# Overflow blocks of a mixture of experts: 32 tokens on four column tiles in place of 64 on two

## The chip, the cores and the metric

The kernel runs on one core of a Trainium2 chip. The metric is the device time of one execution in microseconds (us). Before the change three runs took 2112.33, 2118.11 and 2120.79 us, median 2118.11.

## What is computed

The program is one transformer block (gated token mixer, then a mixture of 32 experts) followed by a second block of two layers (pooling and gated delta rule, each with a feed-forward part). There are 256 tokens of width 1024, all in fp32. The part that the change touches is the mixture of experts:

```python
logits = (xt @ w_router + b_router)            # 256 tokens, 32 experts
top_logits, top_idx = lax.top_k(logits, 4)     # each token goes to 4 experts
top_w = jax.nn.softmax(top_logits, axis=-1)
# for each expert e and the tokens that chose it:
gate, up = jnp.split(xb @ w_gu[e] + b_gu[e], 2, axis=-1)   # 1024 -> 2 x 1024
gate = jnp.minimum(gate, 7.0); up = jnp.clip(up, -7.0, 7.0)
act = (up + 1) * (gate * jax.nn.sigmoid(1.702 * gate))
y[token] += top_w * (act @ w_dn[e] + b_dn[e])              # 1024 -> 1024
```

The number of tokens of an expert depends on the data. With the inputs of this case the router gives experts 2, 16, 27 and 29 more than 64 tokens: 90, 99, 89 and 78. Expert 21 has exactly 64, all others fewer.

## The kernel before

Every engine has its own program, and they meet through semaphores. TensorE (PE) multiplies, VectorE (DVE) makes selection matrices and the clipped activations, ScalarE (ACT) makes the sigmoid and copies, and SyncE (SP) issues the loads of the experts' weights: 12 units of 1 MiB for each expert (8 of gate and up, 4 of down), 384 in all, in a fixed order. The 8 slots of the gate-and-up weights hold one expert's; the down weights have two sets of 4 slots. A slot is loaded again when PE has used it in the expert's last block (`w_used`).

The loop `experts` (L614 to L628) runs on PE, DVE and ACT alike: 16 turns of two experts (j = 0, 1). For each expert the engine reads its number of tokens (L620) and runs an inner loop over b = 1, 2, 3 (L621). A turn with more than 64·b tokens runs `overflow`, a block of 64 tokens. Any other turn only waits until the engine's own earlier steps are done, adds the steps it skips to the semaphore, and goes on (L627). Then `last_block` handles tokens 0 to 63, for every expert. An overflow block comes ahead of it and uses the same resident weights.

A block on PE: the bias (L1171), then gate and up (L1182): for each of 8 slices of 128 inputs four matmuls of 512 columns, 64 tokens stationary, so that the array works as two column tiles of 64. Then the scatter of the previous block's result (L1231), a transposition of the selection matrix (L1207) and of the activations (L1199), and down (L1220), 16 matmuls of 512 columns, two tiles again. An overflow block gathers its tokens first (L1163), while `last_block` gathers those of the next pair (L1155). On DVE a block is limit (L2420, L2421), product with the sigmoid (L2425), the activations (L2429) and the copy of their transposition (L2434); an overflow block begins with the slots (L2401, L2408) and the copy of the gathered tokens (L2413). On ACT it is the sigmoid (L1790), the copy of the transposed selection (L1794) and that of the result (L1799).

An fp32 matmul of the program is two weight loads and two matmuls in the trace.

Of the kernel before, what the change touches and what calls it, by code (L numbers as in the profile page):

```python
# [8 lines left out]
I32 = mybir.dt.int32  # L9
# [4 lines left out]
P = 128  # L14
# [6 lines left out]
KCH = 64  # L21
BLK = 64
EG = 2

PE_MAIN = ("gate_up", "scattered", "next_gathered", "act_T0", "act_T1", "spread_T")
PE_OVER = ("gathered", "gate_up", "scattered", "spread_T", "act_T0", "act_T1", "down")
# [3 lines left out]
DVE_OVER = ("slots0", "slots1", "spread0", "spread1", "tokens", "gate_min", "up_clip", "gated", "act0", "act1",  # L32
            "act_T0", "act_T1")
ACT_FIRST = ACT_OVER = ("sigmoid", "spread_T", "down")
ACT_SECOND = ("sigmoid", "staged_in", "spread_T", "down")

def build(nc, A, out):
# [17 lines left out]
    GTAPS = A["gdn_conv_2"].shape[1]  # L55
    NBLK = S // BLK
    assert NT == 2 and D == 1024 and HEADS == ND and NG == ND and NE == 32

    ctx = ExitStack()
    with ctx:  # L60
# [28 lines left out]
        level = sb("level", [P, 6, P])  # L89
        slot_row = sb("slot_row", [P, NBLK, 2, BLK])  # L90
        slot_int = g2_bc[:, 0:NBLK * 2 * BLK].bitcast(I32)
        inv_pos = sb("inv_pos", [P, 16])
# [471 lines left out]
        pad_end = apad[:, :, :].rearrange("p m t -> p (m t)")[:, len(WINDOWS) * 3 * P:]  # L564
        xg_o = pad_end[:, 0:512].rearrange("p (d s) -> p d s", s=BLK)
        slots_o = pad_end[:, 512:640].rearrange("p (t s) -> p t s", s=BLK)
        bgu_parts = w7[0:96, 1024:2048].bitcast(BF16)
# [12 lines left out]
        class Steps:  # L580
# [3 lines left out]
            def __init__(self, sem_, mains, over, base):  # L584
                self.sem, self.base, self.over_len = sem_, base, len(over)
                overs = (NBLK - 1) * len(over)
                self.first = [j * overs + sum(len(m) for m in mains[:j]) for j in range(EG)]
                self.per = EG * overs + sum(len(m) for m in mains)
                self.main = [{n: overs + i + 1 for i, n in enumerate(m)} for m in mains]
                self.over = {n: i + 1 for i, n in enumerate(over)}  # L590

            def did(self, eng, where, step, pairs_ago=0):

                g, j, b = where
                base = self.base + self.first[j] - pairs_ago * self.per
                if isinstance(b, int):
                    eng.wait_ge(self.sem, g * self.per + (base + self.main[j][step]))
                else:
                    eng.wait_ge(self.sem, g * self.per + b * self.over_len + (base - self.over_len + self.over[step]))

            def started(self, eng, where, less=0):

                g, j, b = where
                base = self.base + self.first[j] - less
                if isinstance(b, int):
                    eng.wait_ge(self.sem, g * self.per + (base + (NBLK - 1) * self.over_len))
                else:
                    eng.wait_ge(self.sem, g * self.per + b * self.over_len + (base - self.over_len))

# [79 lines left out]
        def _(pool):  # L689
# [38 lines left out]
            for i in range(6):  # L728
# [5 lines left out]
                masked(v, [[2 * s, k], [0, s]], s - 1, -1, ALU.is_ge, 0.0)  # L734
            link(nc.gpsimd.iota(slot_int, pattern=[[BLK, NBLK], [0, 2], [1, BLK]], base=0,
                                channel_multiplier=0))
            link(nc.gpsimd.tensor_copy(slot_row[:, :, :, :].rearrange("p b r s -> p (b r s)"), slot_int))
            link(nc.gpsimd.iota(slot_int[:, 0:16], pattern=[[1, 16]], base=1, channel_multiplier=0))
# [112 lines left out]
        def _(pe):  # L851
# [307 lines left out]
            def gather(s_):  # L1159

                for d in range(ND):
                    for t in range(NT):
                        ins = mm(bX[:, d * BLK:(d + 1) * BLK], h2_tok[:, t, d * P:(d + 1) * P], s_[:, t, :],  # L1163
                                 start=t == 0, stop=t == NT - 1)
                step(ins)
# [8 lines left out]

            def gate_and_up(w, x, last):

                for kt in range(ND):
# [6 lines left out]
                    if kt == ND - 1:  # L1184
                        step(ins)
                    elif last:
                        ins.then_inc(w_used, 1)

            def weights(w, u):
# [20 lines left out]

            def down(w, last):
                for n, v in enumerate(DN_ORDER):
# [9 lines left out]
                    if last:  # L1222
                        ins.then_inc(w_used, 1)
                    elif n == 3:
                        step(ins)

# [26 lines left out]
            def overflow(w):  # L1253
                DV.did(pe, w, "slots1")
                AC.started(pe, w, less=1)
                gather(slots_o)
                gate_up_bias()
                DV.did(pe, w, "tokens")
                gate_and_up(w, lambda kt: xg_o[:, kt, :], False)
                AC.started(pe, w)  # L1260
                scatter(spread_T, y_blk)
                spread_transposed(w, spread)
                activation_T(w, 0, bG)
                activation_T(w, 1, bU)
                down(w, False)

            def last_block(w):
# [3 lines left out]
                if j == 0:  # L1271
                    AC.did(pe, (w[0], EG - 1, 0), "staged_in", pairs_ago=1)
                gate_and_up(w, lambda kt: xg[kt // UK][:, kt % UK, j * BLK:(j + 1) * BLK], True)
                AC.started(pe, w)
# [7 lines left out]
                spread_transposed(w, spread)  # L1282
                down(w, True)

# [368 lines left out]
        def _(act):  # L1653
# [134 lines left out]
            def act_block(w, st, y):  # L1788
                DV.did(act, w, "gate_min")
                f(g_sig, g_min, ACT.Sigmoid, scale=SWIGLU).then_inc(moe_act, 1)  # L1790
                if isinstance(w[2], int) and w[1] == EG - 1:
# [232 lines left out]
        def _(dve):  # L2024
# [371 lines left out]
            def find_slots(dst, e, b):  # L2396

                row = slot_row[:, 0, 0, :] if isinstance(b, int) else \
                    slot_row[:, bass.ds(b, 1), 0, :].rearrange("p o s -> p (o s)")
                for t in range(NT):  # L2400
                    step(v.tensor_scalar(dst[:, t, :], row, place[:, t, bass.ds(e, 1)], None, ALU.is_equal))  # L2401

            def find_spread(dst, e, b):

                row = slot_row[:, 0, :, :] if isinstance(b, int) else \
                    slot_row[:, bass.ds(b, 1), :, :].rearrange("p o r s -> p (o r) s")
                for t in range(NT):
                    step(v.tensor_scalar(dst[:, t, :].rearrange("p (r s) -> p r s", r=2), row,  # L2408
                                         place[:, t, bass.ds(e, 1)], gate_of[:, t, bass.ds(e, 1)],
# [7 lines left out]

            def limited(w):
                PE.did(dve, w, "gate_up")
                step(v.tensor_scalar(g_min, banks[5][:, :], LIMIT, None, ALU.min))  # L2420
                step(v.tensor_scalar(u_clip, banks[6][:, :], LIMIT, -LIMIT, ALU.min, ALU.max))  # L2421

            def gated(w):
                AC.did(dve, w, "sigmoid")
                step(v.tensor_tensor(g_act, g_min, g_sig, ALU.mult))  # L2425
                DV.did(dve, w, "gated")
                for i in range(2):
                    cs = slice(i * 256, (i + 1) * 256)
# [9 lines left out]
            for e in range(EG):  # L2438
                for t in range(NT):
                    n[0] += 1  # L2440
                    v.tensor_scalar(slots[:, t, e * BLK:(e + 1) * BLK], slot_row[:, 0, 0, :],
                                    place[:, t, e:e + 1], None, ALU.is_equal).then_inc(dve_step, 1)
# [12 lines left out]
            def overflow(w):  # L2455
# [4 lines left out]
                PE.did(dve, w, "gathered")  # L2460
                copy_tokens(xg_o)
                limited(w)
                gated(w)
                copy_act_T(w)

            def last_block(w):
# [5 lines left out]
                find_spread(spread, e + j, 0)  # L2472
                limited(w)
                gated(w)
                PE.did(dve, w, "next_gathered")
# [471 lines left out]
```

## Time and profile before

| | us |
|---|---|
| median of three runs (lowest, highest) | 2118.11 (2112.33, 2120.79) |
| the profiled execution's own time | 2111.71 |
| its span, first to last instruction | 2110.0 |
| PE busy | 1948.9 (92%) |
| DVE, ACT, POOL busy | 908.0, 469.5, 70.5 |
| first bias matmul of the experts to the end of the last down matmul | 362.6 to 1383.0 |

The experts take about 1020 of the 2110 us. The last line is read from the list of PE's instructions in order of time. A busy PE is not PE at its peak, since a matmul's record is longer than the distance to the next one. Register, branch and semaphore instructions aren't counted as busy; rows named PEldq or PEq are those of PE's sequencer.

### The profile page before, as it was taken

Reading aid. Unit: us, or ns where it says so; the run is one execution under the profiler, and the core shown is the slowest. Engines: PE = TensorE matmul, PEld = TensorE weight load, DVE = VectorE, ACT = ScalarE, POOL = GpSimd, SP = SyncE. Lnnn points to the kernel's source line nnn. Section 1 sums busy time; section 2 is a strip of 40 time slices with the busy share of each in tenths; the row PEclk is TensorE's granted clock in tenths of the full one; section 3 lists DMA queues with packets and bytes.
Section 4 is the critical chain, followed back from the end, with each engine's and each line's share of the span. In section 5 each row is a group of like instructions: output and inputs, shape, how many; then the busy total and the mean of one; then the engine's idle time right before and its main releaser. Section 6 shows DMA issues by size and latency. Waiting matters only on the chain. (4 is left out here: it accounts for less than half of the span.)

```text
span 2110.0 us, 28553 instructions
## 1 busy us (share of the span) xinstructions
PE 1948.9 (92%) x10917; PEld 1222.1 (58%) x10918; DVE 908.0 (43%) x1444; ACT 469.5 (22%) x557; POOL 70.5 (3%) x128
## 2 busy tenths in 40 slices
PE   4999896999999999999999999989999998999998
PEld 2859774433333333333333333358987997878986
DVE  3799644111111111111111121176556787876554
ACT  2223101000000000100000000024543643334542
POOL 2000002000000000000000000010000000020000
PEclk9999997999999999999999999999999989999999
DMA  9794834959999999899999985936555620054552
GB/s 360 246 324 156 300 126 146 417 216 422 421 422 422 422 422 422 332 423 422 422 422 422 408 344 226 401 107 213 180 198 164 202 96 1 1 173 162 189 190 80
DMA packets 143604, 581.37 MB, mean 276 GB/s; under 512 B 10520, under 2 KB 12552, under 8 KB 94281
## 3 DMA queue, kind: packets, MB, share of 16 engines
q1 hardware_dynamic: 136384, 564.43, 68.6%
q0 software_dynamic: 3040, 11.02, 1.7%
q10 hardware_dynamic: 4105, 4.86, 0.7%
q8 instruction: 54, 0.88, 0.2%
q14 instruction: 21, 0.17, 0.0%
HBM read 579.23 MB, written 1.05 MB: 275 GB/s over the span
## 5 line engine op out<-in xcount | busy, mean ns | idle before, releaser
L1182 PE MATMUL bank<-ring,area 128*64 128x512 f32 x2048 | 459.2, 597 | 28.0 <-DMA ring<-in_w_gu 27.6
L1182 PEld LDWEIGHTS bank<-ring,area 128*64 128x64 f32 x2048 | 144.0, 137 | 325.3 <-issue 235.5
L924 PE MATMUL bank<-area_r,ring_r 128*128 128x256 f32 x992 | 282.6, 285 | 9.3 <-DVE area_r L2155 7.1
L926 PE MATMUL bank<-area_r,ring_r 128*128 128x256 f32 x992 | 281.5, 284 | 0.0
L927 PE MATMUL bank<-area_r,ring_r 128*128 128x256 f32 x992 | 281.5, 284 | 0.0
L289 DVE TENSOR_TENSOR ring_r<-ring,ring_r 128x2048 fp32r<-128x2048 f32 x90 | 205.8, 2291 | 149.8 <-ACT ring_r L286 148.1
L2420 DVE TENSOR_SCALAR area<-bank 128x512 f32<-128x512 f32 x36 | 24.9, 692 | 539.6 <-PE bank L1182 539.6
L286 ACT ACTIVATE ring_r<-ring 128x2048 fp32r<-128x2048 f32 x92 | 175.7, 1913 | 179.4 <-PE bank L927 152.2
L924 PEld LDWEIGHTS bank<-area_r,ring_r 128*128 128x128 f32 x992 | 191.3, 193 | 12.1 <-DVE area_r L2155 7.3
L1220 PE MATMUL bank<-area 128*64 128x512 f32 x864 | 192.5, 594 | 0.6 <-DVE area L2434 0.5
L926 PEld LDWEIGHTS bank<-area_r,ring_r 128*128 128x128 f32 x992 | 191.3, 193 | 0.0
L927 PEld LDWEIGHTS bank<-area_r,ring_r 128*128 128x128 f32 x992 | 191.2, 193 | 0.0
L1790 ACT ACTIVATE area<-area 128x512 f32<-128x512 f32 x36 | 22.7, 631 | 532.6 <-DVE area L2420 532.6
L1220 PEld LDWEIGHTS bank<-area 128*64 128x64 f32 x864 | 62.5, 137 | 115.7 <-issue 112.1
L924 PE MATMUL bank<-ring_r,area_r 128*128 128x512 f32 x304 | 118.8, 391 | 1.0 <-DVE area_r L2302 1.0
L926 PE MATMUL bank<-ring_r,area_r 128*128 128x512 f32 x304 | 118.3, 389 | 0.0
L927 PE MATMUL bank<-ring_r,area_r 128*128 128x512 f32 x304 | 118.3, 389 | 0.0
L2185 DVE SCALAR_TENSOR_TENSOR area<-apad,cols,area 128x256 f32<-128x256 f32 x240 | 96.1, 479 | 0.3 <-DVE area L2085 0.2
L1155 PEld LDWEIGHTS bank<-area 128*128 128x128 f32 x544 | 64.6, 195 | 26.0 <-issue 13.9
L1494 PE MATMUL bank<-area 128*128 128x128 f32 x560 | 69.9, 285 | 10.0 <-issue 5.4
L1799 ACT ACTIVATE area<-bank 128x512 f32<-128x512 f32 x36 | 21.5, 597 | 247.3 <-PE bank L1220 247.3
L1494 PEld LDWEIGHTS bank<-area 128*128 128x128 f32 x560 | 66.9, 198 | 13.1 <-issue 7.3
(341 smaller groups left out, 2177.8 us busy)
## 6 DMA issues: line engine op xcount, KB each, us to landing
ring<-in_w_gu SPq DMA_DIRECT2D x256, 1024.0 KB, 21.1
area<-in_w_dn SPq DMA_DIRECT2D x96, 1024.0 KB, 21.0
ring<-in_mlp_w SPq DMA_DIRECT2D x64, 1024.0 KB, 5.4
ring<-in_w_dn SPq DMA_DIRECT2D x32, 1024.0 KB, 19.5
ring<-in_w_in SPq DMA_DIRECT2D x24, 1024.0 KB, 6.3
ring<-in_gdn_w_in SPq DMA_DIRECT2D x16, 1024.0 KB, 5.5
area<-in_w_mod SPq DMA_DIRECT2D x12, 1024.0 KB, 8.6
ring<-in_w_mod SPq DMA_DIRECT2D x8, 1024.0 KB, 17.1
```

The lines of the kernel that those rows point to most:

```text
L286: nc.scalar.activation(unit_high(i), raw, ACT.Copy).then_inc(w_high, 1)
L289: nc.vector.tensor_tensor(unit_low(i), raw, unit_high(i), ALU.subtract).then_inc(w_split, 1)
L924: ins = mm(out_, a_[0], b_[0], start=start, stop=False)
L926: mm(out_, a_[0], b_[1], start=False, stop=False)
L927: return mm(out_, a_[1], b_[0], start=False, stop=stop)
L1155: ins = mm(bk[:, d * P:(d + 1) * P], h2_tok[:, t, (UK * dh + d) * P:(UK * dh + d + 1) * P], slots[:, t, :], start=t == 0, stop=t == NT - 1)
L1182: ins = mm(bk[hf * BLK:(hf + 1) * BLK, :], x(kt), block_u[:, c:c + BANK], start=False, stop=kt == ND - 1)
L1220: ins = mm(bT[hf * BLK:(hf + 1) * BLK, :], actT[:, 2 * i + k, fh * BLK:(fh + 1) * BLK], block_u[:, c:c + BANK], start=n == 0 and k == 0, s ...
L1494: return lambda bk, i, h: mm(bk[:, i * P:(i + 1) * P], l[:, h, :], r[:, h, :], start=True, stop=True)
L1790: f(g_sig, g_min, ACT.Sigmoid, scale=SWIGLU).then_inc(moe_act, 1)
L2185: v.scalar_tensor_tensor(acc[:, m, :], apad[:, m, j:j + S], col("conv_w", j * ND + m), acc[:, m, :], ALU.mult, ALU.add).then_inc(conv_step, 1)
L2420: step(v.tensor_scalar(g_min, banks[5][:, :], LIMIT, None, ALU.min))
```

## The change

`BLK` stays 64 for `last_block`. Overflow blocks have the new width `OBLK` = 32, and the inner loop runs over b = 2 to 7 (six turns in place of three), with `n_tok - b * OBLK > 0` as its condition. In an overflow block PE works as four column tiles of 32: gate and up is 64 matmuls of 256 columns in place of 32 of 512, and in down the two halves of the contraction go to tiles of their own, whose sums the scatter adds. The activations of a block are then 128 partitions by 256, so that DVE and ACT handle 256 elements in each operation in place of 512, and two transpositions do in place of four. `last_block` is unchanged.

```diff
-                    with eng.Fori(1, NBLK) as b:
-                        with eng.If(n_tok - b * BLK > 0):
+                    with eng.Fori(OVER0, OVER1) as b:
+                        with eng.If(n_tok - b * OBLK > 0):
                             overflow((g, j, b))
                         with eng.Else():
 
                             steps.started(eng, (g, j, b))
                             eng.sem_inc(steps.sem, steps.over_len)
                     last_block((g, j, 0))
...
+    OVER0, OVER1 = BLK // OBLK, S // OBLK
...
+            def over_bias():
+
+                for part, bk in ((0, bG), (1, bU)):
+                    for q in range(4):
+                        c = part * D + q * (D // 4)
+                        mm(bk[q * OBLK:(q + 1) * OBLK, 0:D // 4], expert_sel[:, 0:OBLK], bgu_parts[:, c:c + D // 4],
+                           start=True, stop=False)
+
+            def over_gate_and_up(w):
+
+                for kt in range(ND):
+                    block_u = weights(w, kt)
+                    for part, bk in ((0, bG), (1, bU)):
+                        for q in range(4):
+                            c = part * D + q * (D // 4)
+                            ins = mm(bk[q * OBLK:(q + 1) * OBLK, 0:D // 4], xg_o[:, kt, :], block_u[:, c:c + D // 4],
+                                     start=False, stop=kt == ND - 1)
+                step(ins)
+
+            def over_activation_T(w):
+
+                DV.did(pe, w, "act")
+                pairs = e_act[:, 0:D // 4].rearrange("p (f k) -> p k f", k=2)
+                for k in range(2):
+                    ins = mm(bG[:, k * P:(k + 1) * P], pairs[:, k, :], ident[:, :], is_transpose=True,
+                             start=True, stop=True)
+                step(ins)
+
+            def over_down(w):
+
+                DV.did(pe, w, "act_T")
+                for n, v in enumerate(DN_ORDER):
+                    block_u = weights(w, NGU + n)
+                    for k in range(2):
+                        for hf in range(2):
+                            r, c = (2 * hf + k) * OBLK, k * D + hf * BANK
+                            ins = mm(bT[r:r + OBLK, :], actT[:, k, v * OBLK:(v + 1) * OBLK],
+                                     block_u[:, c:c + BANK], start=n == 0, stop=n == 3)
+                step(ins)
...
             def overflow(w):
                 DV.did(pe, w, "slots1")
                 AC.started(pe, w, less=1)
                 gather(slots_o)
-                gate_up_bias()
+                over_bias()
                 DV.did(pe, w, "tokens")
-                gate_and_up(w, lambda kt: xg_o[:, kt, :], False)
+                over_gate_and_up(w)
                 AC.started(pe, w)
                 scatter(spread_T, y_blk)
                 spread_transposed(w, spread)
-                activation_T(w, 0, bG)
-                activation_T(w, 1, bU)
-                down(w, False)
+                over_activation_T(w)
+                over_down(w)
...
                 PE.did(dve, w, "gathered")
-                copy_tokens(xg_o)
-                limited(w)
-                gated(w)
-                copy_act_T(w)
+                step(v.tensor_copy(xg_o, banks[4][:, 0:ND * OBLK].rearrange("p (d s) -> p d s", s=OBLK)))
+                limited(w, D // 4)
+                gated(w, D // 4)
+                PE.did(dve, w, "act_T")
+                step(v.tensor_copy(actT[:, 0:2, :], banks[5][:, 0:2 * P].rearrange("p (j s) -> p j s", s=P)))
```

The rows of `place` numbers that the slots are compared with, the step counts of the semaphores and the sigmoid's width follow from this.

PE's program at the start of the overflow block of the first expert of a pair, before: the count is read, the loop entered, the condition tested, and then come gather (L1163), bias (L1171) and the first slices of gate and up.

```order
988 L620 TENSOR_LOAD counts
989 L620 ISA x2
990 L621 UNCONDITIONAL_BRANCH
991 L621 ISA
992 L622 COMPARE_AND_BRANCH
994 L608 ISA
995 L1163 MATMUL bank4<-apad,area 128x64 x16
996 L1171 MATMUL bank5<-area,expert_sel 64x512 x2
997 L1171 MATMUL bank6<-area,expert_sel 64x512 x2
1000 L1182 MATMUL bank5<-ring,apad 64x512 x2
1001 L1182 MATMUL bank6<-ring,apad 64x512 x2
```

The same place now, where gate and up is L1207 and the bias L1197:

```order
992 L625 COMPARE_AND_BRANCH
994 L611 ISA
995 L1166 MATMUL bank4<-apad,area 128x32 x16
996 L1197 MATMUL bank5<-area,expert_sel 32x256 x4
997 L1197 MATMUL bank6<-area,expert_sel 32x256 x4
1000 L1207 MATMUL bank5<-ring,apad 32x256 x4
1001 L1207 MATMUL bank6<-ring,apad 32x256 x4
```

The order is the same; each pair of matmuls of 512 columns has become four of 256. A pair's loop has 296 matmuls in PE's program before and 372 after. What a turn without a block executes stands at the end of PE's overflow block, before:

```order
1032 L1220 MATMUL bank7<-area 64x512 x8
1033 L622 UNCONDITIONAL_BRANCH
1034 L608 ISA
1035 L624 UNCONDITIONAL_BRANCH
1036 L621 REGISTER_ALU
1037 L621 COMPARE_AND_BRANCH
1038 L606 ISA
```

And now:

```order
1031 L1228 MATMUL bank7<-area 32x512 x8
1032 L625 UNCONDITIONAL_BRANCH
1033 L611 ISA
1034 L627 UNCONDITIONAL_BRANCH
1035 L624 REGISTER_ALU
1036 L624 COMPARE_AND_BRANCH
1037 L609 ISA
```

The instructions of a turn are the same ones; they are executed six times for an expert in place of three.

## Rows read from the trace of the kernel before

**Rows 1.** The page, clock and memory traffic in 40 slices of 52.75 us.
```profile
PEclk9999997999999999999999999999999989999999
...
GB/s 360 246 324 156 300 126 146 417 216 422 421 422 422 422 422 422 332 423 422 422 422 422 408 344 226 401 107 213 180 198 164 202 96 1 1 173 162 189 190 80
```

**Rows 2.** PE in order of time, 476 to 534 us: start, length, line, [idle before].
```profile
477.15 0.61 PE L1171 MATMUL bank<-area,expert_sel 96*64 96x512 bf16 x4
477.58 13.91 PE L1182 MATMUL bank<-ring,area 128*64 128x512 f32 x64
...
503.91 0.62 PE L1171 MATMUL bank<-area,expert_sel 96*64 96x512 bf16 x4
...
530.37 0.61 PE L1171 MATMUL bank<-area,expert_sel 96*64 96x512 bf16 x4
```

**Rows 3.** The bias line L1171, 605 to 818.15 us: ns min/median/max, first and last start.
```profile
L1171 PEld LDWEIGHTS bank<-area,expert_sel x31: 106/107/112, 610.4 to 818.1; 96*64 96x64 bf16 x31
```

**Rows 4.** PE in order of time around expert 2's overflow block, 414 to 452 us.
```profile
419.58 3.79 PE L1163 MATMUL bank<-apad,area 128*128 128x64 f32 x32
423.29 0.62 PE L1171 MATMUL bank<-area,expert_sel 96*64 96x512 bf16 x4
424.24 13.95 PE L1182 MATMUL bank<-ring,apad 128*64 128x512 f32 x64 [0.32 <-DVE apad L2413]
438.12 1.99 PE L1231 MATMUL bank<-area 64*128 64x512 f32 x8
...
445.41 3.61 PE L1220 MATMUL bank<-area 128*64 128x512 f32 x16
450.69 0.62 PE L1171 MATMUL bank<-area,expert_sel 96*64 96x512 bf16 x4 [1.67 <-DVE area L2401]
```

**Rows 5.** Turns without a block, L627, 720 to 730 us, then 445 to 452 us.
```profile
L627 PEldq EVENT_SEMAPHORE  x3: 51/51/51, 726.3 to 728.5; - x3
...
L627 PEldq EVENT_SEMAPHORE  x2: 51/51/51, 449.1 to 450.2; - x2
```

**Rows 6.** PE in order of time, 700 to 762 us.
```profile
728.99 0.62 PE L1171 MATMUL bank<-area,expert_sel 96*64 96x512 bf16 x4 [0.18 <-DVE area L2401]
```

**Rows 7.** Instructions by line, DVE and PE.
```profile
L2420 DVE TENSOR_SCALAR area<-bank 128x512 f32<-128x512 f32 x36 | 24.9, 692 | 539.6 <-PE bank L1182 539.6
...
L2434 DVE COPY area<-bank 128x256 f32<-128x256 f32 x72 | 26.9, 414 | 1.0 <-PE bank L1199 1.0
```

**Rows 8.** Line L1038, 121 to 126 us, then L1163, 418 to 425 us.
```profile
L1038 PE MATMUL bank<-area,cond x24: 592/592/617, 121.4 to 124.5; 128*32 128x512 f32 x24
L1038 PE MATMUL bank<-norm_bc,cond x8: 592/592/617, 121.5 to 124.5; 128*32 128x512 f32 x8
...
L1163 PE MATMUL bank<-apad,area x32: 275/275/323, 419.6 to 423.1; 128*128 128x64 f32 x32
```

**Rows 9.** Stretches: length, busy us of PE, PEld, DVE, ACT, POOL; clock; DMA share, GB/s.
```profile
97.00:100.00 3.00, 0.05 (x4) 0.08 (x8) 2.86 (x7) 0.00 (x0) 0.00 (x0) 1.00 0.27 101
...
100.50:103.90 3.40, 3.40 (x24) 1.07 (x19) 3.40 (x10) 0.00 (x0) 0.00 (x0) 0.50 0.00 0
...
1892.50:1894.70 2.20, 0.04 (x1) 0.07 (x1) 1.43 (x2) 2.20 (x3) 0.33 (x1) 1.00 0.71 199
...
1895.90:1899.30 3.40, 3.40 (x10) 2.66 (x9) 0.00 (x0) 0.00 (x0) 0.00 (x0) 0.50 0.96 353
...
450.70:453.70 3.00, 3.00 (x16) 1.14 (x18) 0.98 (x5) 1.28 (x1) 0.00 (x0) 1.00 0.00 0
```

**Rows 10.** Branches of PE's sequencer, whole run (L622: condition; L618: back to next pair).
```profile
L622 PEldq COMPARE_BRANCH  x100: 77/208/2143, 357.9 to 1355.3; - x100
...
L618 PEldq COMPARE_BRANCH  x17: 76/208/412, 356.1 to 1378.6; - x17
```

**Rows 11.** DMA queues, 340 to 405 us, then 470 to 1380 us: packets, MB, share.
```profile
q8 instruction: 6, 0.10, 0.6%
...
q14 instruction: 2, 0.02, 0.0%
```

More of the change, by code:

```diff
@@ L22 @@
 BLK = 64
+OBLK = 32
 EG = 2
 PE_MAIN = ("gate_up", "scattered", "next_gathered", "act_T0", "act_T1", "spread_T")
-PE_OVER = ("gathered", "gate_up", "scattered", "spread_T", "act_T0", "act_T1", "down")
+PE_OVER = ("gathered", "gate_up", "scattered", "spread_T", "act_T", "down")
 DVE_MAIN = ("spread0", "spread1", "gate_min", "up_clip", "gated", "act0", "act1", "next_tokens", "next_row",
@@ L585, in __init__ @@
                 self.sem, self.base, self.over_len = sem_, base, len(over)
-                overs = (NBLK - 1) * len(over)
+                overs = (OVER1 - OVER0) * len(over)
                 self.first = [j * overs + sum(len(m) for m in mains[:j]) for j in range(EG)]
@@ L598, in did @@
                 else:
-                    eng.wait_ge(self.sem, g * self.per + b * self.over_len + (base - self.over_len + self.over[step]))
+                    eng.wait_ge(self.sem, g * self.per + b * self.over_len + (base - OVER0 * self.over_len + self.over[step]))
             def started(self, eng, where, less=0):
@@ L1173, in gate_up_bias, with gate_and_up @@
                            start=True, stop=False)
-            def gate_and_up(w, x, last):
+            def gate_and_up(w, x):
                 for kt in range(ND):
@@ L1185, in gate_and_up @@
                         step(ins)
-                    elif last:
+                    else:
                         ins.then_inc(w_used, 1)
+            def over_bias():
[30 more added lines that the diff above has]
+                step(ins)
             def weights(w, u):
@@ L1209, in spread_transposed, with down @@
                 step(ins)
-            def down(w, last):
+            def down(w):
                 for n, v in enumerate(DN_ORDER):
@@ L1221, in down @@
                                      block_u[:, c:c + BANK], start=n == 0 and k == 0, stop=n == 3 and k == 1)
[L1222 to L1225, printed above, removed]
+                    ins.then_inc(w_used, 1)
             def scatter(st, y, last=False):
@@ L1282, in last_block @@
                 spread_transposed(w, spread)
-                down(w, True)
+                down(w)
             pe.wait_ge(moe_act, 3)
@@ L1789, in act_block @@
                 DV.did(act, w, "gate_min")
-                f(g_sig, g_min, ACT.Sigmoid, scale=SWIGLU).then_inc(moe_act, 1)
+                wide = BANK if isinstance(w[2], int) else D // 4
+                f(g_sig[:, 0:wide], g_min[:, 0:wide], ACT.Sigmoid, scale=SWIGLU).then_inc(moe_act, 1)
                 if isinstance(w[2], int) and w[1] == EG - 1:
@@ L2396, in find_slots @@
             def find_slots(dst, e, b):
-                row = slot_row[:, 0, 0, :] if isinstance(b, int) else \
-                    slot_row[:, bass.ds(b, 1), 0, :].rearrange("p o s -> p (o s)")
+                row = main_row[:, 0, :] if isinstance(b, int) else \
+                    over_row[:, bass.ds(b, 1), :].rearrange("p o s -> p (o s)")
                 for t in range(NT):
@@ L2403, in find_spread @@
             def find_spread(dst, e, b):
-                row = slot_row[:, 0, :, :] if isinstance(b, int) else \
-                    slot_row[:, bass.ds(b, 1), :, :].rearrange("p o r s -> p (o r) s")
+                row = main_row if isinstance(b, int) else \
+                    over_row[:, bass.ds(b, 1), :].to_broadcast([P, 4, OBLK])
                 for t in range(NT):
-                    step(v.tensor_scalar(dst[:, t, :].rearrange("p (r s) -> p r s", r=2), row,
+                    step(v.tensor_scalar(dst[:, t, :].rearrange("p (r s) -> p r s", s=row.shape[2]), row,
                                          place[:, t, bass.ds(e, 1)], gate_of[:, t, bass.ds(e, 1)],
@@ L2440, in _ @@
                     n[0] += 1
-                    v.tensor_scalar(slots[:, t, e * BLK:(e + 1) * BLK], slot_row[:, 0, 0, :],
+                    v.tensor_scalar(slots[:, t, e * BLK:(e + 1) * BLK], main_row[:, 0, :],
                                     place[:, t, e:e + 1], None, ALU.is_equal).then_inc(dve_step, 1)
@@ L2472, in last_block @@
                 find_spread(spread, e + j, 0)
-                limited(w)
-                gated(w)
+                limited(w, BANK)
+                gated(w, BANK)
                 PE.did(dve, w, "next_gathered")
```

40 lines of the change are left out of this document (21 added, 19 removed).

## The prediction, made before the changed kernel ran

> **What bounds the kernel now.** I read the page's slices first, to see in which stage the change lies. The experts fill slices 7 to 26; memory moves 422 GB/s in most of them and the granted clock is full [rows 1]. Whether PE or memory sets the pace there shows in PE's list in order of time, at the start of each block's bias. Where nothing is waited for, blocks follow each other by 26.76 and 26.46 us, mean 26.6, and gate and up takes 13.91 us [rows 2]. From 610.4 to 818.1 us there are seven such distances, 29.7 us each [rows 3]. That is memory's pace: 12 units of 1.049 MB are 12.58 MB, at 422 GB/s 29.8 us. So PE has 3.1 us of slack per expert, but only while it isn't late. Memory-bound blocks are eight before expert 16's overflow and five before expert 27's, 13 in all; in the others PE catches up after an overflow block, during which the weights' slots couldn't be freed. The waits for memory sum to 13 × 3.1 = 40 us. Every microsecond that PE gains or loses outside those blocks counts in full.
>
> **Turns of the loop.** The change adds three turns without a block for nearly every expert. The last turn's semaphore instruction starts 2.2 us after the first's of three, so that a turn takes PE's sequencer 1.12 us [rows 5]. Now three of them fit: the third's is at 728.5, the next bias starts at 728.99, with PE idle for 0.18 us [rows 5, 6]. The sequencer runs ahead of the queued down matmuls by just what three turns need, and nothing is left to hide three more. Each of the 27 steps between experts without an overflow grows by 3 × 1.12 = 3.4 us: 91 us. The first expert has the same in front: 3.4. DVE and ACT take six turns too, but PE's end last, since DVE's slots wait for PE's turns as it is. PE's distance becomes 26.6 + 3.4 = 30.0 us, just over memory's 29.8: the 40 us of waits go. I take the remainder of them as nothing; it may be 3.
>
> **The blocks.** Run through the reference's router, the inputs give 90, 99, 89 and 78 tokens for experts 2, 16, 27 and 29. At 32 tokens from 64 on, these are 1 + 2 + 1 + 1 = 5 blocks in place of 4. No count lies so near 64 or 96 that rounding would move it, except expert 21's 64, which needs no block in either form unless a token moves.
>
> An overflow block now spans 419.6 to 450.69, 31.1 us [rows 4]. Its parts:
> - Gather, bias, copy of tokens: 419.58 to 424.24, 4.7 us. The gather's 32 records stand 0.11 us apart for 64 columns each [rows 8], so narrower columns don't shorten it; the spacing is the loading of 128 stationary columns. The token copy falls from 512 to 256 elements, from about 692 to 414 ns [rows 7]: −0.3.
> - Gate and up: four column tiles run at once in this trace, 32 records of 512 columns from 121.4 to 124.5, eight groups 0.43 us apart [rows 8], 0.107 us for each. With 256 columns I take half, 0.053; 128 records are 6.9, with the tail 7.1 against 13.95 [rows 4]: −6.9. The bounds are this and 0.11 a record as in the gather, 14.2, no gain. I take the four-tile row, since the shape of the tiles is the same and only the columns are fewer.
> - From its end to down: now 3.7 us (438.19 to 441.93), a chain of DVE, ACT and DVE over 512 elements. By halves it would be 3.0, but PE has 2.4 us of scatter and transposed selection [rows 4], then two transpositions and a copy of 0.4, 3.4 in all: −0.3.
> - Down: 32 records of 512 columns, 0.107 each by [rows 8], 3.4 plus tail 0.2, against 7.1 (from 441.93 to 449.02, its last half in [rows 4]): −3.4.
>
> A block so loses 10.9 us, and is 18.5 long. Behind it stand the turns that are left. They start only when down is done (449.1), 1.1 us apart [rows 5], and the bias waits for them; the gap after down is 1.67 us now with two turns [rows 4] and becomes 5.1 with five. For experts 2, 27 and 29: −10.9 + 3.4 = −7.5, three times −22.5. Expert 16 has a second block: DVE's slots wait for the first one's down, 0.7, and 18.5, 19.2 together; its four turns cost 2.3 more than two. −10.9 + 19.2 + 2.3 = +10.6.
>
> **The clock.** The gaps at the end of every expert are now 0.2 us at most. They become 3.1 to 3.6, and 3.9 to 5.1 after the overflow blocks. After a gap of 3.0 us (97.0 to 100.0) the granted clock is 0.50 for 3.4 us, from 100.5; after one of 2.2 us it is too, from 1895.9 [rows 9]. These levels are 1.2 and 2.4 GHz. I find ten idle gaps of 2.2 us or more in the run, and a stretch at the low level begins in or right after each. After the 1.67 us behind the overflow block the clock stays at 1.00 [rows 4, 9]. So most of the new gaps will be followed by 3.4 us in which half the work is done, 1.7 us lost, less where the gap itself reaches into the stretch. Bounds: none of 31, 0; all at 1.7, 53. I take 25 of 31 at 1.5: +38. Memory has nothing to hide it with, since PE is the bound by then.
>
> **Sum.** 91 + 3.4 − 22.5 + 10.6 − 40 + 38 = +80.5 us. Against the profiled execution's own time of 2111.7 that is 2192; that execution is 6.4 us under the median of 2118.1, which would give 2199. I predict 2195. Outside the experts nothing changes that any stage waits for.
>
> **A rule against the loop.** The condition's branch on PE takes 208 ns in the median and 2143 at most; the branch back over the whole pair, 76 to 412 [rows 10]. The queue that brings PE's program moves six packets around the first pair and none during the later ones [rows 11], so the loop's code stays at hand after its first pass. The Trainium skill, "Runtime: NRT & Kernel Launch", Instruction fetch mechanics, gives PE an instruction memory of 128 KiB, but also says that a taken branch whose target isn't in the current two-page window forces a fetch. By that, a loop of six packets would miss at each jump, and the trace disagrees: the long branch back costs no more than the short ones. The changed pair has 372 matmuls in place of 296, a quarter more code. If six packets were all that is kept, jumps would miss again.
>
> **Rivals.**
> - *The clock holds.* The gaps repeat, but between them PE is busy for 26 us. Same sum without its last term: +42.5, 2154 to 2161. Against it stand all ten long gaps. Chance 0.17.
> - *The turns hide, and the kernel is faster.* Place: the sequencer under the down matmuls. If it entered the turns earlier, since the queue takes more, they would cost nothing, no gap would open, and the blocks' −10.9 × 4 + 19.2 = −24 would be left, of which memory-bound stretches take a few back: −20, 2092. With t the cost of a turn that shows, the loss is about 56·t (3t for 14 late experts, for the first, for three after blocks, 2t for expert 16, none for the 13 with slack), so it decides below 0.4 us a turn. The trace has 1.12 and an idle of 0.18, which says that the cover is used up. Chance 0.05.
> - *Four tiles don't run abreast at 256 columns.* Each of five blocks is 7 longer in gate and up and up to 3.4 in down: +52 on the forecast, 2245. Against it: L1038. Chance 0.06.
> - *The loop's code no longer stays.* One jump per expert at 2143 in place of 208 ns: 32 × 1.9 = 61 us more, 2255, twice that with two jumps. This is the rule's case, priced from [rows 10]. Chance 0.07.
> - The forecast itself: 0.62. Something else of either sign: 0.03.
>
> The range is 2152 to 2215: its lower end is the rival of the steady clock, its upper one all gaps at 1.7 us, taken from the median. About 0.5% (11 us) can be told from no change. Faster 0.06, same 0.03, slower 0.91.
>
> **What would show it.** PE's list of the changed kernel: biases 30 us apart plus what the clock takes, 31 to 32 where a low stretch follows; PE idle of 3.1 to 3.6 us before nearly every bias, with a turn as the releaser; six semaphore instructions of a turn 1.12 us apart; almost no waits of gate and up for the weights; memory's traffic under 422 GB/s in all of the stage; the page's clock below 9 tenths in the experts' slices; in five overflow blocks gate and up of 7.1 us and down of 3.6. The prediction is wrong if biases stand under 29.9 us apart (turns hidden), if the clock is 1.00 throughout the experts (its term gone), or if overflow gate and up takes 14.

## The result: 5.5% slower, and the profile after

The changed kernel takes 2234.47 us in the median of four runs (2228.16 to 2238.63), the one before 2117.73 (2112.33 to 2120.79); ratio 1.0552, 95% interval 1.0519 to 1.0585. The forecast was 2195 with 2152 to 2215: the direction and the mechanism hold, the time lies 20 us above the range. The profiled execution has a span of 2236.9 us and took 2238.63, the slowest of its four, while the profiled one of before (2111.71) was faster than all four timed ones of its kernel, so that the two profiles differ by 126.9 us and the medians by 116.7. Of all executions below, one (of the kernel with three turns, 2260.92 us at a mean granted clock of 0.83 in place of 0.97) was a slow one, and the ratios leave it out.

The page of the changed kernel, first PE's busy share and the granted clock in 40 slices of 55.9 us, then traffic, then gate and up of the last blocks:

```profile
PE   4999878888988898988898889898999998999998
...
PEclk9999896899999999999999999999999998999999
...
GB/s 361 246 303 133 281 120 212 352 236 398 391 388 389 412 386 380 170 326 379 396 399 390 393 248 394 238 273 115 200 188 193 188 164 1 1 114 168 186 195 87
...
L1185 PE MATMUL bank<-ring,area 128*64 128x512 f32 x2048 | 502.4, 653 | 0.0
L1185 PEld LDWEIGHTS bank<-ring,area 128*64 128x64 f32 x2048 | 163.0, 153 | 330.0 <-issue 328.7
```

None of the experts' slices has 422 GB/s any more; [rows 1] have it nearly throughout, and gate and up never waits for it: before, that line was idle 27.6 us for the weights, now nothing. Its mean matmul is 653 ns against 597. The clock's row in tenths hides what happens, since it rounds down and the same 9 stands for 1.00 and 0.92; a window query is needed. PE in order of time, 474 to 560 us:

```profile
489.51 3.61 PE L1263 MATMUL bank<-area 128*64 128x512 f32 x16
496.23 1.06 PE L1174 MATMUL bank<-area,expert_sel 96*64 96x512 bf16 x4 [3.11 <-PEq L630]
497.08 15.00 PE L1185 MATMUL bank<-ring,area 128*64 128x512 f32 x64
...
517.27 7.09 PE L1263 MATMUL bank<-area 128*64 128x512 f32 x32
527.88 1.07 PE L1174 MATMUL bank<-area,expert_sel 96*64 96x512 bf16 x4 [3.52 <-DVE area L2441]
528.72 16.24 PE L1185 MATMUL bank<-ring,area 128*64 128x512 f32 x64
```

The gaps ahead of the bias are the forecast 3.1 and 3.5 us; before there was none at 503.91 and 530.37 [rows 2]. But gate and up takes 15.00 and 16.24 in place of 13.91. The sequencer's turns (L630, 521 to 528 us), six, 1.12 us apart:

```profile
L630 PEldq EVENT_SEMAPHORE  x6: 51/51/51, 521.8 to 527.4; - x6
```

The clock around two gaps, columns as in [rows 9]; the last row is nearly the whole range of the experts:

```profile
524.40:527.90 3.50, 0.02 (x2) 0.03 (x3) 0.28 (x2) 0.60 (x1) 0.00 (x0) 0.81 1.02 424
527.90:533.40 5.50, 5.50 (x16) 1.86 (x18) 0.97 (x5) 1.28 (x1) 0.00 (x0) 0.50 0.95 380
533.50:537.00 3.50, 3.50 (x18) 1.14 (x16) 0.00 (x0) 0.00 (x0) 0.00 (x0) 1.00 0.82 276
557.30:560.40 3.10, 0.05 (x2) 0.06 (x4) 0.32 (x2) 0.58 (x1) 0.00 (x0) 1.00 1.01 420
560.70:564.10 3.40, 3.40 (x12) 1.02 (x10) 0.00 (x0) 0.00 (x0) 0.00 (x0) 0.50 1.02 424
...
380.00:1480.00 1100.00, 970.20 (x5070) 385.79 (x5068) 175.11 (x451) 87.83 (x141) 0.65 (x1) 0.92 0.87 351
```

After the gap of 3.1 us the clock is at 1.2 GHz for 3.4 us. With the gap of 3.5 it is low from inside the gap (the mean of 0.81 puts the fall at 526.6) to 533.4, 6.8 us. Each of the 31 gaps ahead of a last block, from the second expert on, has a low stretch in or behind it: 17 of 3.4 us, 13 of 6.8, and one of 10.2 at a gap of 8.7 us. Of the 26 gaps of 3.1 to 3.5 us, 11 have the long one.

**Where the 126.9 us of the profiles are.** I take from PE's list each expert's last block, from bias to the end of down (26.62 us where nothing disturbs it), and what lies between two of them.

| part | before | after | difference |
|---|---|---|---|
| start of the experts | 362.6 | 371.9 | +9.4 (3.4 are turns) |
| 27 steps between experts without an overflow | 1.6 | 94.7 | +93.1 |
| 4 steps with overflow blocks | 124.0 | 120.8 | −3.3 |
| excess of the 32 last blocks over 26.62, waits for memory | 40.9 | 0 | −40.9 |
| the same, low clock | 2.0 | 67.7 | +65.7 |
| after the experts | 727.0 | 729.9 | +2.9 |

The profile shows 27.6 of the 40.9 us as idle, since a matmul's record is longer than the distance to the next one.

### The profile page after: what moved, and what is told of

It is laid out like the page before. It is cut to its first block and busy times, and to the rows that moved or that the text cites. A ratio compares the mean times of both kernels' runs of the same rounds, so it can differ in the third digit from the quotient of the medians.

```text
span 2236.9 us, 31252 instructions
## 1 busy us (share of the span) xinstructions
PE 1996.7 (89%) x11393; PEld 1254.6 (56%) x11394; DVE 903.7 (40%) x1446; ACT 471.2 (21%) x561; POOL 70.8 (3%) x129
## 5 line engine op out<-in xcount | busy, mean ns | idle before, releaser
L1185 PE MATMUL bank<-ring,area 128*64 128x512 f32 x2048 | 502.4, 653 | 0.0
L1185 PEld LDWEIGHTS bank<-ring,area 128*64 128x64 f32 x2048 | 163.0, 153 | 330.0 <-issue 328.7
L2461 DVE TENSOR_SCALAR area<-bank 128x512 f32<-128x512 f32 (+1 forms) x37 | 24.3, 656 | 552.7 <-PE bank L1185 507.2
L1263 PE MATMUL bank<-area 128*64 128x512 f32 x768 | 171.1, 594 | 0.1
L1830 ACT ACTIVATE area<-area 128x512 f32<-128x512 f32 (+1 forms) x37 | 22.2, 601 | 623.8 <-DVE area L2461 623.8
L1174 PE MATMUL bank<-area,expert_sel 96*64 96x512 bf16 x128 | 31.0, 579 | 121.1 <-DVE area L2441 61.9
L1263 PEld LDWEIGHTS bank<-area 128*64 128x64 f32 x768 | 55.5, 137 | 102.5 <-issue 98.9
L1174 PEld LDWEIGHTS bank<-area,expert_sel 96*64 96x64 bf16 x128 | 5.6, 130 | 149.2 <-DVE area L2441 75.9
L2448 DVE TENSOR_SCALAR area<-slot_row,place,gate_of 128x128 f32<-128x128 f32 (+1 forms) x74 | 22.2, 342 | 158.8 <-PEq L630 158.8
L1158 PEld LDWEIGHTS bank<-area 128*128 128x128 f32 x544 | 65.3, 197 | 25.9 <-issue 13.7
```

The lines of the kernel that those rows point to most:

```text
L1158: ins = mm(bk[:, d * P:(d + 1) * P], h2_tok[:, t, (UK * dh + d) * P:(UK * dh + d + 1) * P], slots[:, t, :], start=t == 0, stop=t == NT - 1)
L1174: mm(bk[hf * BLK:(hf + 1) * BLK, :], expert_sel[:, :], bgu_parts[:, (2 * part + hf) * BANK:(2 * part + hf + 1) * BANK], start=True, stop=F ...
L1185: ins = mm(bk[hf * BLK:(hf + 1) * BLK, :], x(kt), block_u[:, c:c + BANK], start=False, stop=kt == ND - 1)
L2461: step(v.tensor_scalar(g_min[:, cs], banks[5][:, cs], LIMIT, None, ALU.min))
```

## The experiments

Each was timed together with the kernel before, whose medians were 2115.5 to 2116.8 us in these rounds, and ratios are to that. Lines moved by an edit are named by what they do.

**Three turns, narrow blocks.** `OVER1` is 5, so that the loop runs over b = 2 to 4.

```diff
-    OVER0, OVER1 = BLK // OBLK, S // OBLK
+    OVER0, OVER1 = BLK // OBLK, 5
```

> The changed kernel with its loop cut to three turns (b = 2 to 4, enough for the 99 tokens of the largest expert, not for inputs with over 160). Theory A (the turns make the loss: 3.4 us of sequencer time per expert, and a lower clock after each gap): the gaps between experts are 0.2 us again, the clock is 1.00 in the experts, waits for memory come back (about 13 blocks of 3 us), five narrow blocks of some 19.4 us stand in place of four of 29.4, and the time is 2098 to 2105. Rival B (the narrow blocks themselves cost more than they give, by four tiles at once or by their larger code): the time stays over 2118 although the gaps are gone.

2118.08 us, ratio 1.0008 (0.9993 to 1.0023). The gaps and the 116 us are gone, so the loss is the three added turns'. But the gain of 11 to 18 us that theory A wanted didn't come either: the time is the one that rival B named, so the narrow blocks take back what they give. The trace says how, in two ways (expert 2's block, then expert 27's):

```profile
425.97 4.49 PE L1166 MATMUL bank<-apad,area 128*128 128x32 f32 x32
430.39 0.62 PE L1197 MATMUL bank<-area,expert_sel 96*32 96x256 bf16 x8
431.07 9.34 PE L1207 MATMUL bank<-ring,apad 128*32 128x256 f32 x128
...
1205.41 7.85 PE L1207 MATMUL bank<-ring,apad 128*32 128x256 f32 x96
1213.74 1.07 PE L1207 MATMUL bank<-ring,apad 128*32 128x256 f32 x16 [0.47 <-DMA ring<-in_w_gu]
1216.23 1.07 PE L1207 MATMUL bank<-ring,apad 128*32 128x256 f32 x16 [1.42 <-DMA ring<-in_w_gu]
```

Narrow gate and up takes 9.3 us here (8.4 and 9.6 in the two others that don't wait for weights), not 7.1. And experts 16 and 27 come at the end of stretches that memory sets: their narrow block uses up the weights faster than they arrive and waits for them itself. The clock of this kernel in the first of the two blocks:

```profile
425.97:428.80 2.83, 2.83 (x28) 2.83 (x26) 0.00 (x0) 1.88 (x2) 0.00 (x0) 1.00 1.01 423
428.80:435.60 6.80, 6.74 (x61) 3.90 (x64) 0.42 (x1) 0.00 (x0) 0.00 (x0) 0.50 0.67 282
435.70:440.00 4.30, 4.30 (x84) 2.47 (x80) 0.00 (x0) 0.00 (x0) 0.00 (x0) 1.00 0.00 0
```

It falls in the middle of a gather in which PE's records have no gap.

**Six turns, wide blocks.** The kernel before with its loop over six turns; the last three are never taken.

```diff
+    TURNS = 6
...
-                    with eng.Fori(1, NBLK) as b:
+                    with eng.Fori(1, 1 + TURNS) as b:
```

The step counts and the row of slot numbers follow from it.

> The kernel before with 64-token blocks, its loop run over six turns, of which the last three never have a block (the row of slot numbers is stored once and broadcast). Theory A: the whole loss and more is in the turns. 27 steps between experts grow by 3.4 us (92), the four after blocks by 3.4 (14), the first by 3.4, the waits for memory go (-40), and the low clock after 31 gaps costs 2.1 each (65 to 70): +135, 2250. Rival B (a part of the loss is the narrow blocks' or their code's): +90 or less, 2210.

2246.64 us, ratio 1.0632 (1.0613 to 1.0651). Turns alone cost 131 us; theory A's 135 is met, rival B's 90 isn't. The narrow blocks give back some 12 by the medians, 14 if each kernel is set against the one before of its own round. The gap and the slow gate and up are those of the changed kernel, without a narrow block anywhere:

```profile
494.92 1.06 PE L1172 MATMUL bank<-area,expert_sel 96*64 96x512 bf16 x4 [3.14 <-PEq L628]
495.77 16.52 PE L1183 MATMUL bank<-ring,area 128*64 128x512 f32 x64
```

The last blocks exceed 26.62 us by 68.3 us together, against 67.7 there.

**Work in the gap.** Four matmuls behind the last block's down, into a bank that isn't read before it is overwritten:

```diff
                 down(w)
+                for _ in range(4):
+                    mm(bU[:, :], ident[:, :], level[:, 0:4, :].rearrange("p i c -> p (i c)"), start=True, stop=True)
```

> The changed kernel with four matmuls of 128x512 (fp32, 0.85 us each, 3.4 us together) put behind down in every last block, into a bank that is free there; their result is not used. The distance between two experts keeps its 30.0 us at full clock. Theory C (what lengthens the blocks by 2.1 us each beyond the gap is the clock that falls after PE's idle time): with PE busy in the gap the clock stays at 1.00, gate and up is 13.9 us again, and the time falls by 65 to 75, to 2160 to 2170. Rival D (the blocks are longer for another reason, such as PE and memory meeting in the same weights): the blocks stay 28.7 long and the time stays near 2234.

2232.65 us, ratio 1.0569 (1.0546 to 1.0592), practically the changed kernel's time, and not the 2165 expected. PE's list of this kernel settles it all the same:

```profile
523.37 3.70 PE L1324 MATMUL bank<-level,ident 128*128 128x512 f32 x8
528.67 0.62 PE L1174 MATMUL bank<-area,expert_sel 96*64 96x512 bf16 x4 [1.60 <-DVE area L2443]
529.12 13.91 PE L1185 MATMUL bank<-ring,area 128*64 128x512 f32 x64
...
555.24 3.70 PE L1324 MATMUL bank<-level,ident 128*128 128x512 f32 x8
560.16 0.62 PE L1174 MATMUL bank<-area,expert_sel 96*64 96x512 bf16 x4 [1.23 <-PEq L630]
```

Gate and up is back at 13.91 and the clock at 1.00 from 500 to 940 us, as theory C says, and the excess of the last blocks falls from 67.7 to 13.1 us:

```profile
500.00:940.00 440.00, 416.50 (x2167) 170.44 (x2162) 71.55 (x184) 36.65 (x58) 0.00 (x0) 1.00 0.92 372
```

The time stays because the next block comes later: an idle of 1.2 to 1.6 us is left behind the filling, and the distance grows to 31.5 and 31.8 us. The steps between experts without an overflow take 141.8 us in place of 94.7, those with one 130.0 in place of 120.8. One loss was exchanged for another of the same size. That the filling holds up the turns themselves, since the sequencer reaches them only when it is queued too, is the likely reading and wasn't tested.

**One test ahead of the loop, narrow blocks.**

```diff
+                    with eng.If(n_tok - BLK > 0):
+                        with eng.Fori(OVER0, OVER1) as b:
...
+                    with eng.Else():
+                        eng.wait_ge(steps.sem, g * steps.per + (steps.base + steps.first[j]))
+                        eng.sem_inc(steps.sem, (OVER1 - OVER0) * steps.over_len)
```

> The changed kernel with one test ahead of the loop: an expert of at most 64 tokens skips all six turns with a single wait and one addition to the semaphore. Theory A: 28 experts have no gap and full clock; only behind the overflow blocks there are still four or five turns (5.0 us and a low clock, 7 us each). The waits for memory come back. 2110 to 2122, about the kernel before. Rival B: as for the kernel with three turns, over 2125.

2130.66 us, ratio 1.0072 (1.0055 to 1.0089), 9 above the range of theory A and in rival B's. Of the 27 steps without overflow 26 have no gap (−0.17 us each, since the bias overlaps the end of down); the first has 3.45. What is left are the turns behind the blocks, with 1.4 to 3.0 us of low clock behind each, and low clock in the blocks.

**A gather of 64 columns.** Three turns, and each slot column twice:

```diff
-                        ins = mm(bX[:, d * OBLK:(d + 1) * OBLK], h2_tok[:, t, d * P:(d + 1) * P], s_[:, t, :],
+                        ins = mm(bX[:, d * BLK:(d + 1) * BLK], h2_tok[:, t, d * P:(d + 1) * P], s_[:, t, :],
```

> Narrow blocks, loop cut to three turns, and the gather of an overflow block streams 64 columns again (each slot column twice; the second half is not used). In the kernel with three turns every narrow block has a stretch at half clock that begins during or just after its gather or inside gate and up. Theory E (the gather of 32 columns leaves the array mostly idle although PE's records are gapless, and that lowers the clock): with 64 columns the low stretches of the blocks go, 1.2 to 2.5 us for each of five, and the time is 6 to 10 us under the kernel with three turns, 2108 to 2112. Rival F (the four 32-wide tiles or the pauses around them lower it): low stretches stay, 2118.

2106.15 us, ratio 0.9951 (0.9938 to 0.9964), 2 under theory E's range and far from rival F's 2118. Expert 2's block in this kernel, in PE's order:

```profile
426.87 3.79 PE L1166 MATMUL bank<-apad,area 128*128 128x64 f32 x32
...
431.26 7.11 PE L1207 MATMUL bank<-ring,apad 128*32 128x256 f32 x128 [0.27 <-DVE apad L2505]
...
446.79 0.62 PE L1174 MATMUL bank<-area,expert_sel 96*64 96x512 bf16 x4 [1.65 <-DVE area L2444]
```

The clock over its gather and its gate and up is 1.00 in both:

```profile
426.87:430.50 3.63, 3.63 (x34) 3.63 (x32) 0.00 (x0) 1.88 (x2) 0.00 (x0) 1.00 1.00 420
431.26:438.30 7.04, 7.04 (x128) 4.21 (x128) 0.00 (x0) 0.00 (x0) 0.00 (x0) 1.00 0.43 178
```

Gate and up is 7.11, as forecast for full clock. The gather itself is no longer than with 32 columns (3.75 us at full clock). Taken over the kernels with narrow blocks, a low stretch begins during the gather or within 1.3 us of its end at 18 of 20 gathers of 32 columns (the changed kernel, three turns, work in the gap, one test) and at none of 15 of 64 (this kernel, the same with a test, and six turns; the kernel with the turns ahead isn't counted, since four of its five gathers come behind a gap). The two exceptions are expert 16's first block, in the kernel with three turns and in the one with work in the gap. The one low stretch left in a block here is also in expert 16's first, 859.8 to 863.2 us, where gate and up waits for weights.

**The loop from the highest block down, with the test and the wide gather.** It holds for any number of tokens.

```diff
+                        with eng.Fori(0, OVER1 - OVER0) as b:
+                            with eng.If(n_tok + b * OBLK - (OVER1 - 1) * OBLK > 0):
```

> Valid for any number of tokens: experts of at most 64 tokens skip the loop with one test, the six turns run from the highest block down, so that turns without a block come ahead of the blocks, where the queued down matmuls of the previous expert cover most of them, and the gather streams 64 columns. Theory A: no gap for 28 experts, for the four others a gap of about 3 us ahead of the block in place of 4 to 5 behind it, and none behind. 2108 to 2118, under the kernel that skips with the turns behind (2131) by 12 or more. Rival: the turns ahead aren't covered, since the sequencer gets to them only when down is queued: 2122 or more.

2119.82 us, ratio 1.0011 (0.9997 to 1.0026), a little outside the range: as fast as before, no faster. It is 11 under the kernel with the turns behind. The gather alone brings 12 in the kernels with three and with six turns, so nothing here shows that the order of the turns gains anything. The steps of experts 2 and 29 come to 28.0 and 28.2 us where three turns and the same gather have 19.8, with 4.6 and 4.9 us of idle ahead of the gather and a low clock of 10 to 14 us around it: the turns ahead open a gap too.

**Four and five turns, wide blocks.** The same edit as for six.

> 64-token blocks with four turns, the last one never with a block. Theory A with the clock: the gap between experts becomes 1.0 to 1.3 us, which in the trace of before lowered nothing, so the clock stays at 1.00 there. 14 experts that were late grow by 1.12, the first too, four after blocks by 1.14 and by a low stretch each (gap 2.8): +21 and +6 to +8, 2136 to 2146. If the clock falls at this gap as well, 2160 or more.

2128.28 us, ratio 1.0064 (1.0043 to 1.0085). Gaps of 0.9 and 1.3 us; the clock is 1.00 from 470 to 850 us, and gate and up 13.91:

```profile
508.74 0.62 PE L1172 MATMUL bank<-area,expert_sel 96*64 96x512 bf16 x4 [1.26 <-DVE area L2402]
509.19 13.91 PE L1183 MATMUL bank<-ring,area 128*64 128x512 f32 x64
536.28 0.62 PE L1172 MATMUL bank<-area,expert_sel 96*64 96x512 bf16 x4 [0.90 <-PEq L628]
```

It is 8 under the range. The larger part of that is memory: in the profiles the 27 steps grow by 27.9 us and the waits for memory fall by 24.9, which leaves 3.0 where the forecast has 15.7 (14 late experts at 1.12). The gaps of 2.8 us behind the blocks lowered the clock at one of four, not at each, which saves a few us more.

> 64-token blocks with five turns. Gaps of 2.0 to 2.4 us between experts. Sequencer alone: 14 late experts and the first by 2.24, four after blocks by 2.3, +43. If such gaps lower the clock in a part of the cases (theory A), +20 to +35 on top, 2175 to 2195; if they lower it always and for as long as those of 3.5 us, 2210; if never, 2160.

2193.66 us, ratio 1.036 (1.0341 to 1.0379), at the top of the range. Gaps of 2.0 and 2.4 us; after one of them:

```profile
520.25 1.07 PE L1172 MATMUL bank<-area,expert_sel 96*64 96x512 bf16 x4 [2.38 <-DVE area L2402]
521.10 15.11 PE L1183 MATMUL bank<-ring,area 128*64 128x512 f32 x64
550.50 0.79 PE L1172 MATMUL bank<-area,expert_sel 96*64 96x512 bf16 x4 [2.01 <-PEq L628]
```

The granted clock behind the first of them is 0.50 for 3.3 us:

```profile
520.20:523.50 3.30, 3.25 (x10) 1.16 (x12) 1.04 (x6) 0.96 (x1) 0.00 (x0) 0.50 1.02 425
```

Of its last blocks 27 are longer by 1.5 to 1.9 us, most by 1.71, half of 3.4. They are the four behind overflow blocks (gaps of 3.9 us) and 23 of the 26 with gaps of 2.0 to 2.4; the other three have no low stretch. So by the medians the fourth turn costs 12 us, the fifth 65, the sixth 53: a turn's price is 1.12 us per expert less what the waits for memory take up, and from the fifth on nearly every gap adds a stretch of half clock.

**The same test ahead of three turns.** First the kernel before with it, then the narrow one with the gather of 64.

> The kernel before (64-token blocks, three turns) with one test ahead of the loop, so that an expert of at most 64 tokens skips its turns. The turns are nearly hidden there (0.13 to 0.19 us of gap at every second expert, none at the others), so that theory A gives it 0.3 us for each of some 7 late experts and 1 to 2 us at the first two: 0 to 4 us, 2112 to 2117. A rival (even hidden turns cost, by delaying DVE and ACT): 10 us or more.

2113.09 us, ratio 0.9990 (0.9979 to 1.0002): no difference that can be told, and the rival's 10 us is excluded. It is a balance of two small things. The 27 steps are 6.3 us shorter, of which waits for memory take back 3.2. But the gap behind each overflow block is 1.9 us in place of 1.6 to 1.7, and at three of the four the clock falls after it, which it did at none before; it costs 1.7 us each:

```profile
1216.73 0.62 PE L1175 MATMUL bank<-area,expert_sel 96*64 96x512 bf16 x4 [1.90 <-DVE area L2412]
1217.18 15.60 PE L1186 MATMUL bank<-ring,area 128*64 128x512 f32 x64
```

> The version with three turns and the gather of 64 columns, with the same test ahead of the loop. By the same count 0 to 4 us less than without the test (2106): 2102 to 2106.

2103.76 us, ratio 0.9942 (0.9929 to 0.9956), the lowest median here; its interval overlaps that of the same kernel without the test, so a gain by the test itself isn't shown, only that of three turns, gather and test together. It handles up to 160 tokens for an expert, as its loop has three turns.

**Six turns with the gather of 64.**

> The changed kernel with six turns, only its gather streaming 64 columns. If the account of the loss adds up, the low stretches inside the five narrow blocks go (1.2 to 2.5 us each) while those after the gaps stay: 6 to 12 us under the changed kernel, 2222 to 2228.

2222.76 us, ratio 1.0507 (1.0485 to 1.0529). The four steps with blocks take 23.2, 41.2, 23.2 and 23.2 us, 110.8 together, against 120.8 in the changed kernel. The other parts of the table agree within 0.7 us (the last blocks' excess is 67.2), except for the time after the experts, 2.9 lower. So the gather of 32 columns costs 10 us in the profiles and 12 in the medians, 9 if each is set against the kernel before of its own round.

## Why the prediction was wrong, point by point

- *Turns of the loop: right.* 3.4 us for each of 27 steps, 91 in all; the table has 93.1. Of this 3.5 are something else: a branch of the condition at the second expert, on its first pass, took 5.69 us in place of 2.14 [rows 10], and the gap there is 8.7 us. The first expert's 3.4 is in the +9.4; the other 6 were lost ahead of the experts, where the clock was low for longer in this execution (0.92 against 0.94 over the first 362 us). The other kernels whose experts all run six turns start them at 365.5, 367.3 and 371.2 us, so these 6 look like spread between executions; that wasn't tested.

```profile
L625 PEldq COMPARE_BRANCH  x197: 77/208/5691, 363.3 to 1477.7; - x197
```

- *Waits for memory: right.* −40 forecast, −40.9 measured; none remain.
- *The blocks: right as arithmetic, wrong in clock.* The forecast 23.6 and 41.6 us for the steps are 23.2 and 41.2 in the kernel whose clock stays up in the block; gate and up there is 7.1, four tiles abreast as at [rows 8]. In the changed kernel the steps are 26.2, 45.7, 24.4 and 24.4. The −11.9 for all became −3.3, since I took the narrower gather at its length alone, and put what the clock does in a narrow block at nothing. The length didn't change, but with 32 columns in place of 64 for each load the clock fell: 8.6 us that the sum lacks. Gate and up of the five blocks took 8.3 to 9.6 us, where the sign that I named was 7.1.
- *The clock: the step that failed.* "I take 25 of 31 at 1.5: +38", bounds 0 and 53. It is +65.7 in the last blocks, 2.1 us for each of 31. All 31 gaps have a low stretch. The 17 stretches of 3.4 us cost 1.6 each, as priced; the 14 longer ones cost 2.7 each, so that the upper bound of 1.7 per gap was no bound. The trace of before had such lengths to read. Behind the ten idle gaps that I counted stand nine low stretches, and only three are 3.4 us long; three are 6.8, and the others 10.2, 13.7 and 17.1. I priced all by two of the three short ones, those in [rows 9]. (At two of the ten, around 260 and 1727 us, the stretch had begun before the gap, so that "begins in or right after each" was misread.) The one at the first expert, before:

```profile
359.90:366.70 6.80, 4.12 (x12) 1.39 (x14) 1.25 (x6) 0.00 (x0) 0.00 (x0) 0.50 0.48 158
```

  With 2.1 the sum would have been 108 and the time some 2223, 11 under the measured one; 8.6 of these are the narrow gather. The sign "the page's clock below 9 tenths in the experts' slices" was badly chosen: the mean is 0.92, and but for the first two slices the row still says 9.
- *Rivals.* The clock didn't hold; turns didn't hide (0.18 us of idle was the end of the cover, and the fourth turn already costs 12 us); four tiles do run abreast. The loop's code stays: the queue that brings PE's program, q8, moves seven packets around the first pair (350 to 435 us, first line below) and none from 435 to 1500 us, where the second line is the only one of a queue of instructions, and the branch's median is still 208 ns, with 372 matmuls in the pair.

```profile
q8 instruction: 7, 0.11, 0.6%
...
q14 instruction: 2, 0.02, 0.0%
```

  So the two-page rule of the Trainium skill ("Runtime: NRT & Kernel Launch", Instruction fetch mechanics) isn't borne out here either, while the 128 KiB of the same section is compatible with it: seven packets are 0.11 MB. What the larger code seems to cost is the one first jump: it takes 5.6 to 6.6 us in five kernels with narrow blocks, 2.14 before and 0.6 in the kernel with six turns of wide blocks.
- *Where the blocks' gain goes without added turns.* Of the −24 us for the blocks, some 11 come when the gather keeps 64 columns (2106 against 2117). At experts 16 and 27 the narrow block waits 4.4 us each for weights, because memory sets the pace there. With the gather of 32 columns, and the low clock in the block, nothing is left at all (2118).

## What to carry to other kernels

A turn of a loop that does nothing has a price on the sequencer, here 1.12 us on PE; count the turns against the queued work that covers them, and see whether the cover is already used up. When a change opens a repeated gap on PE, price the clock after the gap as well as the gap, and list all low stretches of the trace before choosing a bound, not the two nearest. A test ahead of a rarely needed loop took away most of the loss (2234 to 2131 us), not all of it; the narrow blocks came out ahead of the kernel before only with three turns and the gather of 64 columns (2106, 2104).

## What the runs showed of the hardware

- The granted clock fell to 0.50 inside a gather of 32 streamed columns per loaded 128x128, although PE's busy time had no gap (2.83 of 2.83 us in the stretch before the fall, 6.74 of 6.80 in the low one). It did so in or just behind 18 of 20 such gathers; with 64 columns, as long in time, at none of 15. So PE's busy share alone didn't tell here whether the clock would fall. Why two of the 20 had no fall wasn't tested.
- By the length of the gap ahead of a last block, the clock was low in or behind it at none of 27 of 0.9 to 1.3 us (four wide turns); at none of four of 1.6 to 1.7 (the kernel before); at five of seven of 1.9 (the two kernels with a test and three turns); at 23 of 26 of 2.0 to 2.4 (five wide turns); at one of four of 2.8 (four wide turns); at all 26 of 3.1 to 3.5 (the changed kernel). What decides between equal gaps wasn't tested.
- Four fp32 matmuls of 128x512 queued behind down (3.7 us) moved the next bias from 3.1 and 3.5 us behind down to 4.8 and 5.2: filling a gap that the sequencer makes can move the gap.
